# Differential values as a pair of seven block products, begun together with the gate pair

## The reference, cut to what matters

```python
def second_block(x, mem, g_norm, w_in, diff_lambda, ...):
    for l in range(DEPTH):                       # DEPTH = 2
        x = mixer_layer(x, mem, l, g_norm[l], w_in[l], ...)
    return rmsnorm(x, g_final)

# in the layer: h = rmsnorm(x, g_norm[l])        256 tokens x 1024
# h @ w_in[l]                                    w_in: 1024 x 13312, 26 chunks of 512 columns
# chunks 0..3: q and k of 8 heads x 2 maps, 4..5: v, 6..7: gate of the differential attention
# s = q.k * 64**-0.5 + bias;  p = softmax(s);  o = (p_map0 - lambda * p_map1) @ v
# o is normed by head and multiplied by silu(gate)
```

## Time and profile before

| | us |
|---|---|
| median of 3 runs | 2100.16 (2098.97 to 2100.8) |
| span of the profiled execution | 2098.7 |
| busy TensorE, matmuls | 1828.7 |
| busy VectorE | 690.8 |
| busy ScalarE | 380.8 |
| first product of `w_in`, first layer of block two | 1130.08 |
| first product of `w_in`, second layer of block two | 1610.12 |

### The profile page before, as it was taken

The page is one execution under the profiler, slowest core; times in us unless marked ns, Lnnn a source line. Parts: engine busy times, 40 slices in busy tenths (PEclk is TensorE's granted clock), DMA queues, the critical chain, the costliest instruction groups (busy, mean ns, idle before and its releaser), DMA issues.

```text
span 2098.7 us, 34922 instructions
## 1 busy us (share of the span) xinstructions
PE 1828.7 (87%) x15046; PEld 1214.5 (58%) x15046; DVE 690.8 (33%) x1228; ACT 380.8 (18%) x881; POOL 119.3 (6%) x182
## 2 busy tenths in 40 slices
PE   8998676777688867776778999999999999999998
PEld 5656455545466655555454868646544768746543
DVE  5641110111043211111114043473652043573752
ACT  3511011001013110110012022222211022222221
POOL 1100000000000000000004003000230001100000
PEclk9999888988899998988999999999999999999999
DMA  8599999999999999999999834244456643443331
GB/s 331 181 377 419 420 421 420 420 420 420 420 397 407 420 420 420 420 420 420 420 399 271 223 137 154 95 161 159 133 192 169 161 160 130 132 160 121 130 121 60
DMA packets 156205, 590.69 MB, mean 281 GB/s; under 512 B 16528, under 2 KB 34320, under 8 KB 107024
## 3 DMA queue, kind: packets, MB, share of 16 engines
q1 hardware_dynamic: 147504, 569.53, 70.4%
q0 software_dynamic: 8544, 18.89, 3.7%
HBM read 579.98 MB, written 8.39 MB: 280 GB/s over the span
## 4 chain that ended last, share of the span: by engine, by line
PE 58%; DMA 24%; SPq 10%; DVE 5%; issue 2%; ACT 1%; DVEq 0%; ACTq 0%
DMA ring<-in_moe_w_dram 22%; PE ps L603 14%; PE ps L571 14%; PE ps L582 7%; SPq L1203 6%; PE ps L1479 4%; SPq L1212 2%; PE ps L577 2%; PE ps L1459 2%; SPq L1219 2%; PE ps L1514 2%; PE ps L487 1%; PE ps L1756 1%; PE ps L548 1%; DMA arena<-in_moe_w_dram 1%
## 5 line engine op out<-in xcount | busy, mean ns | idle before, releaser
L1479 PE MATMUL ps<-ring,xT 128*32 128x128 f32 x8192 | 304.7, 307 | 181.2 <-DMA ring<-in_moe_w_dram 174.6
L1479 PEld LDWEIGHTS ps<-ring,xT 128*32 128x32 f32 x8192 | 264.7, 121 | 244.6 <-DMA ring<-in_moe_w_dram 189.7
L571 PE MATMUL ps<-xT,ring 128*128 128x256 f32 x1408 | 310.1, 380 | 0.0
L571 PEld LDWEIGHTS ps<-xT,ring 128*128 128x128 f32 x1408 | 265.3, 190 | 39.8 <-issue 4.9
L2173 DVE TENSOR_TENSOR arena<-arena,ps 128x256 f32<-128x256 f32 x32 | 13.5, 421 | 556.4 <-ACT arena L1850 556.4
L1012 DVE TENSOR_TENSOR ring<-ring 128x2048 f32<-128x2048 f32 x56 | 128.4, 2292 | 154.9 <-PE ps L603 147.7
L1514 PE MATMUL ps<-arena 128*32 128x512 f32 x768 | 118.4, 600 | 33.8 <-DVE arena L2173 30.9
L1142 POOL DMA_DIRECT2D ring<-gap_bias x160 | 96.6, 671 | 807.8 <-DVEq L2346 459.9
L1459 PE MATMUL ps<-arena,x_tm 128*128 128x128 f32 x1024 | 137.8, 291 | 0.0
L1459 PEld LDWEIGHTS ps<-arena,x_tm 128*128 128x128 f32 x1024 | 129.3, 205 | 11.1 <-issue 11.1
L603 PE MATMUL ps<-ring,xT 128*128 128x512 f32 x288 | 130.1, 594 | 1.5 <-ACT arena L761 1.5
(11 more groups left out here) (299 smaller groups left out, 1935.0 us busy)
## 6 DMA issues: line engine op xcount, KB each, us to landing
ring<-in_moe_w_dram SPq DMA_DIRECT2D x287, 1024.0 KB, 26.0
arena<-in_moe_w_dram SPq DMA_DIRECT2D x89, 1024.0 KB, 26.7
ring<-in_w_in_dram SPq DMA_DIRECT2D x44, 2048.0 KB, 8.2
ring<-in_w_in_dram SPq DMA_DIRECT2D x16, 1024.0 KB, 12.2
ring<-in_w_br_diff_dram SPq DMA_DIRECT2D x4, 2048.0 KB, 10.6
ring<-in_w_out_dram SPq DMA_DIRECT2D x4, 2048.0 KB, 8.1
arena<-in_moe_w_dram SPq DMA_DIRECT2D x14, 512.0 KB, 15.0
ring<-in_w_mem_kv_dram SPq DMA_DIRECT2D x3, 2048.0 KB, 18.8
```

Source lines behind the costliest of these rows:

```text
L571: m = nc.tensor.matmul(bank[:, u * T:(u + 1) * T], w[:, k, f * P:(f + 1) * P], xT[:, k, :], start=(k == 0), stop=(k == KD - 1))
L1479: m = nc.tensor.matmul(ps[SL * q:SL * q + SL, g % 2, s * P:(s + 1) * P], xs[:, g % 2, k, s * SL:(s + 1) * SL], w[:, c0:c0 + 2 * P - 1:2], ...
```

## The change

The values' chunks 4 and 5 become a pair too (`VALUES`, 0), and the gate's 6 and 7 move ahead of chunks 0 to 3 (`GATE`, 2). The fourteen block products of both pairs are written out in an order of their own: units 0 and 2 of both on the first token tile, then units 1, 3, 4, 5, 6 of the values and after them those of the gate. `turn_x` stands behind the third product. `begin_pairs` does VectorE's part, with eight `combine_w` and `combine_x` among them. What the PE waits for among the combinations is now a place in a list (`COMBOS`). The gate's first part has a place of its own (`PT3[:, 0, :]`).

```diff
-    plan = [(w[c], None, None) for c in (4, 5, 0, 1, 2, 3, 6, 7)]
+    plan = [(w[c], None, None) for c in (4, 5, 6, 7, 0, 1, 2, 3)]
...
-         if c == ("br_diff", 0) or (c[0] == "w_in" and c[1] in (6, 14, 16, 20, 22, 24))]
+         if c == ("br_diff", 0) or (c[0] == "w_in" and c[1] in (4, 6, 14, 16, 20, 22, 24))]
...
-ORDER = [(0, 0), (1, 0), (0, 1), (1, 1)]
-ORDER += [(i, half) for i in range(2, LASTS) for half in range(HALVES[i])]
+VALUES, GATE = 0, 2
+ORDER = [(VALUES, 0), (VALUES, 2), (GATE, 0), (GATE, 2)]
+ORDER += [(i + u // 4, u % 4) for i in (VALUES, GATE) for u in (1, 3, 4, 5, 6)]
+ORDER += [(i, half) for i in range(4, LASTS) for half in range(HALVES[i])]
...
+COMBOS = [(VALUES, 0), (VALUES, 1), "x", (GATE, 0), (VALUES, 2), (VALUES, 3), (GATE, 1), (GATE, 2), (GATE, 3)]
...
                 if kind == "diff" and h == 0:
-                    wait_taken(pe, l, chunk_of("w_in", 5))
+                    pe.wait_ge(sem("w_ready2"), l * DH + 1)
...
                 if u == 1:
-                    pe.wait_ge(sem("combined"), combined_for(l, i, 0))
+                    pe.wait_ge(sem("combined"), combined_for(l, "diff x" if is_diff(i) else "x"))
                 if u > 2:
-                    pe.wait_ge(sem("combined"), combined_for(l, i, (1, 3, 4, 4)[u - 3]))
+                    pe.wait_ge(sem("combined"), combined_for(l, (i, (0, 2, 3, 1)[u - 3])))
...
-                product(l, 0, 0)
-                product(l, 1, 0, 0, KD // 2)
+                for u in (0, 2):
+                    pair_product(l, VALUES, u)
+                pair_product(l, GATE, 0)
                 turn_x(l, 1)
-                product(l, 1, 0, KD // 2, KD)
+                pair_product(l, GATE, 2)
                 pe.wait_ge(sem("turn_read"), turned[0])
-                product(l, 0, 1)
-                product(l, 1, 1)
+                for i in (VALUES, GATE):
+                    for u in (1, 3, 4, 5, 6):
+                        pair_product(l, i, u)
...
-                take(l, 0, 0)
+                for i in (VALUES, GATE):
+                    copy_product(l, i, 0, first_parts[i])
                 take_x(1)
...
-                combine_x(PAIRS[0])
+                def begin_pairs():
+                    values, gate = pair_outputs(VALUES), pair_outputs(GATE)
+                    combine_w(VALUES, 0)
+                    wait_product_taken(v, l, unit_at(VALUES, 0))
+                    add_product(VALUES, 2, values[0])
+                    combine_w(VALUES, 1)
+                    combine_x(VALUES)
+                    wait_product_taken(v, l, unit_at(GATE, 0))
+                    add_product(GATE, 2, gate[0])
+                    output_done(GATE, 0)
+                    combine_w(GATE, 0)
+                    for i, (o11, o12, o21, o22) in ((VALUES, values), (GATE, gate)):
+                        first_part = first_parts[i]
+                        combine_w(i, 2)
+                        combine_w(i, 3)
+                        wait_product_taken(v, l, unit_at(i, 3))
+                        add_to(o12, o22)
+                        if i == GATE:
+                            gate_pair(i, 6, 0, 0)
+                        add_product(i, 4, first_part)
+                        add_to(o12, first_part)
+                        if i == VALUES:
+                            combine_w(GATE, 1)
+                        else:
+                            output_done(i, 1)
+                            gate_pair(i, 6, 1, 1)
+                        add_product(i, 6, first_part)
+                        add_to(o22, first_part)
+                        if i == GATE:
+                            output_done(i, 3)
+                        wait_product_taken(v, l, unit_at(i, 5))
+                        add_to(o21, first_part)
+                    output_done(GATE, 2)
+                    gate_pair(GATE, 6, 2, 3)
+                    gate_pair(GATE, 6, 3, 2)
+
+                begin_pairs()
```

More of the change, by code:

```diff
@@ L106 @@
 NJOB = len(JOBS)
+DIFF_PAIR = [i for i in PAIRS if PLAN[i][0][0] == "br_diff"][0]
+COMBOS = [(VALUES, 0), (VALUES, 1), "x", (GATE, 0), (VALUES, 2), (VALUES, 3), (GATE, 1), (GATE, 2), (GATE, 3)]
+for _i in PAIRS[2:]:
+    COMBOS += (["diff x"] if _i == DIFF_PAIR else []) + [(_i, j) for j in range(4)]
 MAPS = dict(diff=2, mem=1)
@@ L316, in build @@
         turned_of = dict(diff=oaT, dil=obT, mem=omT, merged=mergedT)
-        KH, COMBINED, TANHS = KD // 2, 2 + 4 * len(PAIRS), 20
+        KH, COMBINED, TANHS = KD // 2, len(COMBOS), 20
         S1, S2, S3x = consts[:, P:P + KH * P], gap_rows[:, :], x_comb[:, 0:KH * P]
         S4_of = [arena[:, AW - 3 * P + k * P:AW - 2 * P + k * P] for k in range(3)] + [x_comb[:, KH * P:]]
-        first_part = S3[:, 2, :]
+        first_parts = {i: PT3[:, 0, :] if i == GATE else S3[:, 2, :] for i in PAIRS}
         S_dil = S3[:, 0:2, :].rearrange("p m k -> p (m k)").rearrange("p (t k) -> p t k", t=TT)
@@ L344, in s4_piece, with combined_for @@
             return x_combined(i)[3][:, k, :] if is_diff(i) else S4_of[k]
-        def combined_for(l, i, n):
-            j = PAIRS.index(i)
-            return l * COMBINED + 1 + 4 * j + (1 if j >= PAIRS.index(chunk_of("br_diff", 0)) else 0) + n
+        def combined_for(l, what):
+            return l * COMBINED + COMBOS.index(what) + 1
         tanh_parts = (S3[:, 0, :], PT3[:, 1, :], PT3[:, 2, :], S3[:, 1, :])
@@ L425, in pair_outputs @@
             c = PLAN[i][0][1]
+            if c == 4:
+                return [dv[:, t, cc * CW:(cc + 1) * CW] for t in range(TT) for cc in range(2)]
             if c == 0:
@@ L818, in act_second @@
             for l in range(DEPTH):
-                take(l, 0, 0)
+                for i in (VALUES, GATE):
+                    copy_product(l, i, 0, first_parts[i])
                 take_x(1)
-                for i, half in ORDER[1:4]:
-                    take(l, i, half)
+                for i in (VALUES, GATE):
+                    _, o12, o21, o22 = pair_outputs(i)
+                    copy_product(l, i, 1, o12)
+                    if i == VALUES:
+                        pair_tanh(l, GATE, 0, 0)
+                    copy_product(l, i, 3, o22)
+                    if i == GATE:
+                        pair_tanh(l, i, 1, 1)
+                    copy_product(l, i, 5, o21)
+                for j, which in ((2, 3), (3, 2)):
+                    pair_tanh(l, GATE, j, which)
                 job_n = 0
                 for i, (chunk, job, after) in enumerate(PLAN[:LASTS - 1]):
-                    if i < 2 or i - 1 in PAIRS:
+                    if i < 4 or i - 1 in PAIRS:
                         continue
```

16 lines of the change are left out of this document (8 added, 8 removed).

## The result

| | before | after |
|---|---|---|
| median, us (16 runs each) | 2100.18 | 2103.5 |
| ratio, 95% interval | | 1.0017 [1.001, 1.0023] |
| span of the profiled execution | 2098.7 | 2101.7 |
| first to first product of `w_in`, layer 1 to layer 2 | 480.04 | 487.40 |
| first product of layer 2 to the end of the span | 488.58 | 485.25 |

The kernel is slower by 3.3 us (2.1 to 4.8). The two stage times are differences of starts in the timelines: 1610.12 - 1130.08 and 2098.7 - 1610.12 before, 1616.45 - 1129.05 and 2101.7 - 1616.45 after. They leave out the expert stages ahead, which came 1.0 us shorter in this profile. The second layer (with all behind it) gained 3.3 us; the first lost 7.4. By the stages alone the change costs 4.0 us, which is also inside the interval of the medians.

What follows compares the result with a forecast made beforehand. TensorE was taken as the bound: -6.4 us over both layers, +6.5 and +2.1 in the first, took the span from 2098.7 to 2100.9, median 2102.4 us. Own range 2099.5 to 2104.5; 8 in 10 from 2093.6 to nearly 2107.0.

Steps and rivals of the forecast that it cites:

- eighth product: In the values, 7 products replace 8, so eight TensorE records of 0.429 us go: -3.43 us a layer.
- wait for `combine_x`: Unit 1 of the values waits on TensorE until VectorE has finished `combine_x`: +1.3 us a layer.
- wait of the first scores: After chunk 3, TensorE waits for ScalarE's copy of the last product before the first scores: +0.8 us a layer.
- first turn of weights: TensorE's stall there goes whole, as the gate pair's VectorE tail no longer precedes the first job: -1.88 us a layer.
- wait for chunk 6: First layer, gate's unit 0: TensorE waits from 1136.94 until the third load lands at 1143.4, +6.5 us (bounds 0 and 11.5).
- clock behind it: After the first layer's load wait, TensorE runs at half clock for a while: +2.1 us (ends 1.5 and 2.8).
- rival A: Chunk 6 lands in time in the first layer, leaving only -6.4 us: 2093.8 us, chance 0.25.
- The argument for the landing: SyncE's queue gets turns by packets; chunk 6, 1024 packets like half of chunk 0, lands when that did, 1143.4.
- B: Bytes count, not packets: chunk 6 lands at 1148.4, its wait is 11.5 us, total 2107.4 us; chance 0.12.
- C: VectorE becomes the bound in the pairs through late combinations, adding 4.6 us: 2107.0 us; chance 0.08.
- D: The exchange at the scores gives nothing because ScalarE is late for the exponentials, +3.8: 2106.2 us; chance 0.05.

Runs made afterwards that it cites:

- e2: The kernel before with only the list of chunks in the new order, values still four plain products: 2097.18 us, ratio 0.9985 to the kernel before.
- e1: The changed kernel with GpSimd's first bias and memory loads issued only once chunk 7 has landed: 2093.35 us, ratio 0.9966 to the kernel before.
- f2: The changed kernel with 8 idle matmuls ahead of the gate's unit 0 in the first layer: 2100.58 us, ratio 1.0006 to the kernel before.
- g1: The changed kernel with chunk 6 loaded as two half loads written in runs of 64 floats: 2108.21 us, ratio 1.0037 to the kernel before.
- f3: The changed kernel with memory keys and values loaded at once and bias tables only after chunk 7 landed: 2094.24 us, ratio 0.9973.
- e4: The changed kernel with the values' unit 3 ahead of unit 1 and the gate's unit 1 behind them: 2103.78 us, ratio 1.0012.

## Why the prediction was right, and where its argument was not

The forecast was +2.2 us, 2102.4; measured were +3.3, 2103.5, inside the forecast's own range, and within 0.2% as it held likeliest. By its own terms, each measured from start to start of products in the timelines, in us:

| term | forecast | measured |
|---|---|---|
| eighth product, a layer | -3.43 | -3.46 |
| wait for `combine_x`, a layer | +1.3 | +1.45 |
| wait of the first scores | +0.8 | +0.84 |
| first turn of weights | -1.88 | -2.02 |
| second layer, to the first turn | -3.2 | -3.20 |
| second layer and all behind it | -3.2 | -3.33 |
| wait for chunk 6 | +6.5 | +7.46 |
| clock behind it | +2.1 | +2.90 |
| first layer, to the first turn | +5.4 | +7.05 |
| whole first layer | +5.4 | +7.36 |

The eighth product's measured value is of the second layer: both pairs took 1666.92 - 1616.45 = 50.47 us there, less 1.45 of waiting and 0.88 of the turn 48.14; values and gate took 28.36 - 0.89 and 24.13 before, 51.60. Chunks 0 to 3 took 55.25 us before (1638.48 to 1693.73) and the scores start 56.09 behind 1666.92 now, of which 0.68 is shown as idle; from the scores to the first turn it was 10.10 us and is 8.08. So the second layer was worked out right, term by term. The last 0.3 us of the first are the longer wait for ScalarE named under e2, which the prediction did not have.

The first layer was priced 2.0 us too low. By the stages the change costs 7.36 - 3.33 = 4.0 us, where 5.4 - 3.2 = 2.2 were forecast; the spans differ by 3.0 only because the expert stages came 1.0 us shorter in the profile after, and the medians' 3.3 has an interval from 2.1 to 4.8. So the total fits the forecast somewhat better than its first-layer terms do. Two small slips stand in its numbers: rival A's time is 2093.8 where it is worked out and 2093.6 in the range, and a landing at 1144 with 2.8 us of clock gives 2103.7, so the upper end of 2104.5 has 0.8 us in it that are not accounted for. The measured 2103.5 lies inside either way.

*Chunk 6* was the decisive step and held: it landed at 1143.3 where 1143.4 was said, TensorE stopped where it was said, and e1 gives back the whole of it. Against full pace the wait is 1.0 us longer than said. The layer began 1.0 us earlier in that profile, for TensorE and for the load (issued at 1107.0, not 1107.9), but the load took 36.3 us from its issue instead of 35.5. *The clock* was undersized: of the two cases of the earlier trace rows, 2.8 and 1.5 us, the longer one came, and f2 shows that the loss is all clock. *The wait for `combine_x`* lacked the 0.32 us from the end of the operation to TensorE's start; `combine_x` itself ended 0.1 us earlier behind the turn than was worked out.

*The argument for the landing* was half wrong, though its number was right. The prediction said that the queue gets its turn by packets and carried over from the half loads both the number of packets of chunk 6 (1024) and the share of the queue. The number is as said (1.49 MB in 739 packets are 2 KB each). The share is not: beside the same bias loads whole chunks take turns one for one, half loads two for five (g1 shows that it is the kind of load). The Trainium skill, in "DMA: Bandwidth & Descriptors", section "Queues, rings and completion order", says that an engine alternates between its queues packet by packet. By that rule the trace agrees for whole chunks (292 to 288) and not for half loads (149 to 363), if the profile's packets, rows of 1 or 2 KB, are the packets that the rule means, which no run here shows. The prediction worked out 729 packets for each queue from 1124 to 1139 us by that rule; 739 and 739 came. That this is so close is in part chance: a packet took 0.208 and 0.130 us of an engine (64.0% and 40.0% of 240 us by 739), where 0.231 and 0.098 were put in, and only the sum of the two is nearly the same.

Its second error was to hand this case to rival A, which needs a landing by 1137. In the kernel before SyncE's queue moved 718 packets in the 4.4 us behind 1139, so 332 packets more by 1139 bring the landing forward by 2.0 us, to 1141.4. Forecast and rule led to nearly the same landing, and the prediction set them against each other.

Why did the landing fit when the share did not? Counted from the issue of the layer's first load (1103.96, 1103.02 and 1104.36 us), the packets of SyncE's queue and of GpSimd's were:

| us from the first issue | before, half loads | after, whole chunks | g1, half loads |
|---|---|---|---|
| 14 to 20 | 1123, 32 | 958, 75 | 1129, 34 |
| 20 to 32 | 339, 706 | 578, 577 | 328, 709 |
| 32 to 39.3 | 749, 318 | 528, 399 | 755, 313 |

The whole chunks gain 239 packets on the kernel before in the middle and lose 165 ahead of it and 221 behind it. From 0 to 39.5 us GpSimd's queue had moved 1056, 1052 and 1056 packets and SyncE's 4797, 4702 and 4841: nearly the same work was done by then, only in another order, and the landings came 39.4, 40.3 and 39.3 us behind the first issue. The prediction did not work this out, so that its 1143.4 was met to 0.1 us is in part luck. Why GpSimd's queue gets going more slowly beside half loads, though its first load is issued 14.4 us behind SyncE's in all three, stays open.

*Rivals.* A (in time) fell; e1 and f3 show what it would have needed, the bias loads out of the way. B (bytes count) fell for whole chunks; g1, with halves, is what it would have looked like (the rival gave 2107.4; g1 took 2108.2). C (VectorE the bound) fell for the change as it stands, though e4 shows how near it was: a combination put one place too late costs 1.3 us a layer. D fell: the turn's stall went whole, and e2 confirms the exchange by itself.

## What to carry to other kernels

A product saved is worth what the trace says only if the operand of the reordered work is there. When a change moves a load's first use earlier, read the landing of what stood at that place of the queue, with the traffic of the other queues beside it, and not the time a load takes alone: here 36.3 us, 21.8 with GpSimd's loads held back, and 7.3 and 11.6 for the half loads of the earlier trace rows. In this kernel the bias tables were not needed before the first scores, over 100 us later, and issuing them behind the chunks that TensorE waits for turned +3.3 us into -6.8 by one wait on GpSimd. And where a wait cannot be taken away, idle matmuls in it save what the clock would cost (2.9 us here).

## What the runs showed of the hardware

- Two DMA queues with work shared the engines one packet for one where SyncE's packets were rows of 2 KB (739 to 739 in 15 us), and two for five where they were rows of 1 KB written in runs of 256 B (149 to 363 in 6 us, 142 to 357 in g1).
- A 2 MB load at the third place of its queue landed 21.8 us behind its issue with the other queue empty, 24.4 beside 1 MB in rows of 4 KB, 33.9 beside 2 MB of bias tables in runs of 256 B, 36.3 beside both.
- 7.2 us of idle TensorE brought the granted clock from 1.00 (2.4 GHz) to 0.50 (1.2 GHz), and it took until about 1149.0, 5.6 us behind the restart, to come back; with the same time filled by matmuls on constants it stayed at 1.00.
